# Two blocks on one core: half of x's rows and all of the context's turned by VectorE and ScalarE instead of TensorE

## The reference

```
# first block
u = rmsnorm(x);  proj = u @ w_in
y_f = fourier_mix(proj[:, :1024])            # 4 groups, DFT over positions and channels, then w_fourier
y_a = dilated_attention(q, k, v)             # 8 heads of 128
x = x + concat(y_f, y_a) @ w_out
x = x + square(relu(rmsnorm(x) @ w_up)) @ w_down;   x = rmsnorm(x)
# second block
mod = silu(c) @ w_mod + b_mod                # shift, scale and gate; one set for x, one for the context
hc = rmsnorm(ctx) * (1 + sc1c) + sh1c;  k, v, gates of the context = hc @ w_in2   -> start states
hx = rmsnorm(x) * (1 + sc1) + sh1;      q, k, v, g, low rank, cb, cc, cx = hx @ w_in2
mix = concat(gla(q, k, v, gates, states) * silu(g), cb * conv3(cc * cx)) @ w_out2
x = x + gt1 * mix;   x = x + gt2 * swiglu(modulated rmsnorm(x));   out = rmsnorm(x)
```

## Time and profile before

| what | value |
|---|---|
| median of 3 runs | 2249.17 us (2249.11 to 2249.85) |
| the profiled execution's own time | 2250.41 us |
| its span | 2248.7 us |
| granted TensorE clock | 0.998 of full |
| TensorE, VectorE, ScalarE busy | 99%, 73%, 51% of the span |
| last feed-forward chunk's steps 16 to 31, ScalarE's and VectorE's | about 926 to 1022 us |
| context's blocks k, l, v0, v1 on TensorE | 1021.9 to 1097 us |
| x's blocks on TensorE | 1097 to about 1420 us |

### The profile page before, as it was taken

One profiled execution on the slowest core, in us unless ns is written; L12 is line 12 of the kernel. 1 busy time (PEld: TensorE's weight loads), 2 busy tenths in 40 slices (PEclk: granted clock), 3 DMA queues, 4 the chain that ended last, 5 costly groups with the idle time before them and its releaser, 6 DMA issues.

```text
span 2248.7 us, 28778 instructions
## 1 busy us (share of the span) xinstructions
PE 2230.3 (99%) x10115; PEld 1841.4 (82%) x10115; DVE 1642.7 (73%) x2156; ACT 1149.5 (51%) x1500; POOL 226.6 (10%) x369
## 2 busy tenths in 40 slices
PE   9999999999999999999999999999999999999998
PEld 7888888888888888888878877878888888888886
DVE  7998789988988988998788774656555545555556
ACT  5446457446546645645565744544443344434444
POOL 0111001111111111111011000001110011100110
PEclk9999999999999999999999999999999999999999
DMA  8983678988887898887678663656665666655663
GB/s 310 325 270 123 207 249 297 326 275 296 293 303 271 277 314 279 276 275 259 219 238 256 224 198 113 226 168 203 209 198 191 220 197 203 206 189 189 207 192 124
DMA packets 250109, 527.97 MB, mean 235 GB/s; under 512 B 22258, under 2 KB 22658, under 8 KB 248704
## 3 DMA queue, kind: packets, MB, share of 16 engines
q1 hardware_dynamic: 214256, 405.32, 54.7%
q0 software_dynamic: 33776, 116.17, 15.0%
q10 hardware_dynamic: 1952, 4.85, 0.6%
HBM read 517.87 MB, written 4.21 MB: 232 GB/s over the span
## 4 chain that ended last, share of the span: by engine, by line
PE 96%; DVE 2%; ACT 1%; issue 0%; DMA 0%; ACTq 0%; DVEq 0%; POOLq 0%
PE acc L1981 30%; PE acc L1985 30%; PE acc L1990 30%; PE tp L2053 1%; DVE wlo L1176 1%; PE acc L2004 0%; PE acc L2009 0%; PE acc L2014 0%; PE tp L2367 0%; PE tp L2385 0%; PE tp L2379 0%; PE acc L2037 0%; PE acc L2036 0%; PE acc L2035 0%; PE m L2174 0%
## 5 line engine op out<-in xcount | busy, mean ns | idle before, releaser
L609 ACT ACTIVATE whi<-wring 128x1024 fp32r<-128x1024 f32 x756 | 796.4, 1060 | 930.9 <-PE acc L1990 929.7
L1176 DVE TENSOR_TENSOR wlo<-wring,whi 128x1024 fp32r<-128x1024 f32 x754 | 909.6, 1225 | 439.5 <-ACT whi L609 438.2
L1981 PE MATMUL acc<-whi,xhi 128*128 128x512 f32 x2056 | 556.1, 392 | 0.1
L1985 PE MATMUL acc<-whi,xlo 128*128 128x512 f32 x2056 | 549.8, 389 | 0.0
L1990 PE MATMUL acc<-wlo,xhi 128*128 128x512 f32 x2056 | 549.7, 389 | 0.0
L1985 PEld LDWEIGHTS acc<-whi,xlo 128*128 128x128 f32 x2056 | 386.0, 188 | 80.7
L1990 PEld LDWEIGHTS acc<-wlo,xhi 128*128 128x128 f32 x2056 | 386.0, 188 | 80.4
L1981 PEld LDWEIGHTS acc<-whi,xhi 128*128 128x128 f32 x2056 | 383.2, 188 | 82.4 <-issue 4.7
L1218 DVE SCALAR_TENSOR_TENSOR macc<-mring,csil,macc 128x512 f32<-128x512 f32 x480 | 344.3, 749 | 36.0 <-DMA mring<-w_mod 30.1
L493 POOL DMA_DIRECT2D mring<-w_mod x192 | 139.2, 725 | 1101.2 <-DVE macc L1218 1054.2
L1981 PE MATMUL acc<-whi,ahi 128*128 128x512 f32 x608 | 163.5, 391 | 0.0
(11 more groups left out here) (296 smaller groups left out, 1335.2 us busy)
## 6 DMA issues: line engine op xcount, KB each, us to landing
wring<-w_up SPq DMA_DIRECT2D x216, 512.0 KB, 5.0
wring<-w_down SPq DMA_DIRECT2D x216, 512.0 KB, 5.7
mring<-w_mod POOLq DMA_DIRECT2D x192, 512.0 KB, 5.5
wring<-w_in SPq DMA_DIRECT2D x184, 512.0 KB, 5.0
wring<-w_gate SPq DMA_DIRECT2D x88, 512.0 KB, 4.4
wring<-w_out SPq DMA_DIRECT2D x64, 512.0 KB, 5.0
tmpT<-blk POOLq DMA_DIRECT2D x128, 32.0 KB, 3.2
gbig<-ctx_in POOLq DMA_DIRECT2D x2, 1024.0 KB, 6.5
```

The source lines that it names most:

```text
L609: act.activation(whi[:, piece_slot(c, piece), 0:half], wring[:, g4, piece * half:(piece + 1) * half], ACT.Copy).then_inc(hi_done, 1)
L1176: dve.tensor_tensor(wlo[:, h4, 0:half], wring[:, g4, piece * half:(piece + 1) * half], whi[:, h4, 0:half].bitcast(F32), ALU.subtract).then ...
L1981: pe.matmul(acc[:, 2 * pair + t, :], hi[:, tile, t * P:(t + 1) * P], whi[:, h4, w], start=(tile == starts), stop=False)
L1985: pe.matmul(acc[:, 2 * pair + t, :], lo[:, tile, t * P:(t + 1) * P], whi[:, h4, w], start=False, stop=False)
```

## The change

The context's eight banks and four of x's eight are no longer turned on TensorE. Instead VectorE transposes 32x32 blocks of four tiles at a time (`turn_ctx`, `half_turn`), ScalarE moves 16 pieces of 32 partitions to their places (`move_ctx`, `half_move`), VectorE applies scale and shift in SBUF (`set_ctx`, `half_set`), ScalarE rounds the four tiles (`round_ctx`, `half_round`) and VectorE writes their remainder (`split_ctx`, `half_split`). The context's four sets start at steps 16, 20, 24 and 28, and the last one ends behind k's first two groups. x's tiles 0 to 7 are still turned on TensorE, one bank behind each group from (v0, 2) to (v1, 1); tiles 8 to 15 are turned in h's memory from (v0, 1) to (cc0, 1). TensorE waits for `ctx_lo` at k, and for `row_lo` ahead of groups 2 and 3 of cc0. The convolution's second half moves from (l, 1) and (v0, 2) to (k, 3) and (l, 0), with its strips closer together. The first head's scaling on ScalarE moves ahead of the store of the last projection block.

Of the diff, the changed lines (declarations of semaphores and of views left out):

```
...
+        ctx_pairs = tmpT[:, :, :].rearrange("p a n -> p (a n)"), ctx_placed[:, :]
+        ctx_places = [pair.rearrange("p (k t i b) -> p i k t b", k=KG, t=T, i=4) for pair in ctx_pairs]
+        ctx_tiles = [pair.rearrange("p (k s) -> p k s", k=KG) for pair in ctx_pairs]
+        ctx_strips = strips.rearrange("p j (k t b) -> p j k t b", k=KG, t=T)
...
-        CTX_TURNS = {g: b for b, g in enumerate((20, 22, 24, 25, 26, 28, 29, 30))}
-        BESIDE = ({("k", 0): (("half_norm", 0, 0, 0),), ("k", 1): (("mid_norm", 0, 0, 0),),
+        CTX_TURNED = {16: 0, 20: 1, 24: 2, 28: 3}
+        CTX_MOVES = {17: ((0, 0),), 18: ((0, 1), (0, 2)), 19: ((0, 3),), 21: ((1, 0),), 22: ((1, 1), (1, 2)), 23: ((1, 3),),
+                     25: ((2, 0),), 26: ((2, 1), (2, 2)), 27: ((2, 3),), 29: ((3, 0),), 30: ((3, 1), (3, 2)), 31: ((3, 3),)}
+        CTX_SET, CTX_ROUNDED, CTX_SPLIT = {20: 0, 25: 1, 28: 2}, {21: 0, 26: 1, 29: 2}, {22: 0, 26: 1, 30: 2}
+        BESIDE = ({("k", 0): (("ctx_set", 0, 3, 0), ("ctx_hi", 0, 3, 0), ("half_norm", 0, 0, 0)), ("k", 1): (("ctx_lo", 0, 3, 0), ("mid_norm", 0, 0, 0)),
-                   ("l", 0): (("x_squares", 0, 2, 4),), ("v0", 0): (("x_norm", 0, 0, 0), ("shift_sum", 0, 0, 0)), ("v0", 2): (("x_turn", 0, 0, 0),),
-                   ("v0", 3): (("x_turn", 0, 1, 0), ("x_turn", 0, 2, 0)), ("v1", 0): (("x_turn", 0, 3, 0),),
-                   ("v1", 1): (("x_turn", 0, 4, 0), ("x_turn", 0, 5, 0)), ("v1", 2): (("x_turn", 0, 6, 0), ("x_turn", 0, 7, 0))}, {})
+                   ("l", 0): (("x_squares", 0, 2, 4),), ("v0", 0): (("x_norm", 0, 0, 0), ("shift_sum", 0, 0, 0)), ("v0", 1): (("half_turn", 0, 0, 0), ("half_move", 0, 0, 0)),
+                   ("v0", 2): (("x_turn", 0, 0, 0), ("half_turn", 0, 1, 0), ("half_move", 0, 0, 1)),
+                   ("v0", 3): (("x_turn", 0, 1, 0), ("half_move", 0, 0, 2), ("half_move", 0, 0, 3)),
+                   ("v1", 0): (("x_turn", 0, 2, 0), ("half_set", 0, 0, 0), ("half_move", 0, 1, 0)),
+                   ("v1", 1): (("x_turn", 0, 3, 0), ("half_round", 0, 0, 0), ("half_move", 0, 1, 1)),
+                   ("v1", 2): (("half_split", 0, 0, 0), ("half_move", 0, 1, 2)), ("v1", 3): (("half_move", 0, 1, 3),)}, {})
-            ("cc0", 0): (("stack_gates", 0, 0, 0),), ("cc0", 1): (("beyond", 0, 0, 0),),
+            ("cc0", 0): (("half_set", 0, 1, 0), ("half_round", 0, 1, 0), ("stack_gates", 0, 0, 0)),
+            ("cc0", 1): (("half_split", 0, 1, 0), ("beyond", 0, 0, 0)),
...
-            ("cb1", 2): (("conv_place", 1, 2, 1),), ("cb1", 3): (("conv_place", 1, 2, 2),),
-            ("k", 0): (("conv_place", 1, 2, 3), ("conv_turn", 1, 3, 0)), ("k", 1): (("conv_place", 1, 3, 0),),
-            ("k", 2): (("conv_place", 1, 3, 1),), ("k", 3): (("conv_place", 1, 3, 2),),
-            ("l", 0): (("conv_place", 1, 3, 3),), ("l", 1): (("conv", 1, 1, 0),), ("v0", 2): (("conv", 1, 1, 1),),
+            ("cb1", 2): (("conv_place", 1, 2, 1), ("conv_place", 1, 2, 2)), ("cb1", 3): (("conv_place", 1, 2, 3),),
+            ("k", 0): (("conv_turn", 1, 3, 0),), ("k", 1): (("conv_place", 1, 3, 0), ("conv_place", 1, 3, 1)),
+            ("k", 2): (("conv_place", 1, 3, 2), ("conv_place", 1, 3, 3)), ("k", 3): (("conv", 1, 1, 0),),
+            ("l", 0): (("conv", 1, 1, 1),),
...
                         exponentials(0)
+                        scale_probs(0)
...
+            def scale_probs(hd):
+                act.wait_ge(den_inverted, hd + 1)
+                act.activation(probs[:, S:2 * S], probs[:, S:2 * S], ACT.Copy,
+                               scale=arden[:, hd, 1:2]).then_inc(probs_scaled, 1)
...
-                act.wait_ge(den_inverted, s)
-                act.activation(probs[:, S:2 * S], probs[:, S:2 * S], ACT.Copy,
-                               scale=arden[:, s - 1, 1:2]).then_inc(probs_scaled, 1)
+                else:
+                    scale_probs(s - 1)
...
+            def move_ctx(n, strip):
+                if strip == 0:
+                    act.wait_ge(ctx_turned, T * (n + 1))
+                    if n == 0:
+                        act.wait_ge(relu_lo, KG * MLP_MOVED * MLP_CHUNKS)
+                    elif n >= 2:
+                        act.wait_ge(ctx_lo, n - 1)
+                for i in range(4):
+                    placed_rows = act.activation(ctx_places[n % 2][32 * strip:32 * strip + 32, i],
+                                                 ctx_strips[32 * i:32 * i + 32, strip], ACT.Copy)
+                placed_rows.then_inc(ctx_moved, 1)
+            def round_ctx(n):
+                act.wait_ge(ctx_set, n + 1)
+                act.activation(ahi[:, 4 * n:4 * n + 4, :], ctx_tiles[n % 2], ACT.Copy).then_inc(ctx_hi, 1)
...
                     round_groups(1)
-                    if last and g in CTX_TURNS:
-                        round_modulated(ahi, CTX_TURNS[g], CTX_TURNS[g] + 1)
+                    if last and g in CTX_ROUNDED:
+                        round_ctx(CTX_ROUNDED[g])
+                    for n, strip in CTX_MOVES.get(g, ()) if last else ():
+                        move_ctx(n, strip)
...
+                elif kind == "half_move":
+                    if b == 0:
+                        act.wait_ge(row_turned, T * (a + 1))
+                    for i in range(4):
+                        placed_rows = act.activation(conv_places[a][32 * b:32 * b + 32, i],
+                                                     conv_strips[a][32 * i:32 * i + 32, b], ACT.Copy)
+                    placed_rows.then_inc(row_moved, 1)
+                elif kind == "half_round":
+                    act.wait_ge(row_set, a + 1)
+                    act.activation(xhi[:, 8 + 4 * a:12 + 4 * a, :], conv_tiles[a], ACT.Copy).then_inc(row_hi, 1)
+                        act.wait_ge(row_lo, 2)
...
+            def turn_ctx(n):
+                if n == 0:
+                    dve.wait_ge(u_done, T)
+                    dve.wait_ge(relu_moved, 4 * MLP_MOVED * MLP_CHUNKS)
+                else:
+                    dve.wait_ge(ctx_moved, 4 * n)
+                for t in range(T):
+                    rows = u_g[:, t, n * NB:(n + 1) * NB]
+                    dve.transpose(turned[:, t], rows.rearrange("p (k j b) -> p k j b", k=KG, j=4)).then_inc(ctx_turned, 1)
+            def set_ctx(n):
+                dve.wait_ge(ctx_moved, 4 * (n + 1))
+                for k in range(KG):
+                    tile = ctx_tiles[n % 2][:, k, :]
+                    set_tile = dve.tensor_scalar(tile, tile, ctx_gain(KG * n + k), ctx_shift(KG * n + k), ALU.mult, ALU.add)
+                set_tile.then_inc(ctx_set, 1)
+            def split_ctx(n):
+                dve.wait_ge(ctx_hi, n + 1)
+                dve.tensor_tensor(alo[:, KG * n:KG * (n + 1), :], ctx_tiles[n % 2],
+                                  ahi[:, KG * n:KG * (n + 1), :].bitcast(F32), ALU.subtract).then_inc(ctx_lo, 1)
...
                             set_gain1()
-                    if last and g in CTX_TURNS:
-                        modulate_bank(CTX_TURNS[g], ctx_gain, ctx_shift)
+                    if last and g in CTX_TURNED:
+                        turn_ctx(CTX_TURNED[g])
+                    if last and g in CTX_SET:
+                        set_ctx(CTX_SET[g])
                         done += n
-                    if last and g in CTX_TURNS:
-                        remainder_bank(ahi, alo, CTX_TURNS[g])
+                    if last and g in CTX_SPLIT:
+                        split_ctx(CTX_SPLIT[g])
...
+                elif kind == "half_turn":
+                    dve.wait_ge(u_done, 3 * T)
+                    dve.wait_ge(spill_s, 16)
+                    for t in range(T):
+                        rows = u_g[:, t, D // 2 + a * NB:D // 2 + (a + 1) * NB]
+                        dve.transpose(conv_turns[a][:, t], rows.rearrange("p (k j b) -> p k j b", k=KG, j=4)).then_inc(row_turned, 1)
+                elif kind == "half_set":
+                    dve.wait_ge(row_moved, 4 * (a + 1))
+                    for k in range(KG):
+                        tile = conv_tiles[a][:, k, :]
+                        kt = KT // 2 + KG * a + k
+                        set_tile = dve.tensor_scalar(tile, tile, x_gain(kt), x_shift(kt), ALU.mult, ALU.add)
+                    set_tile.then_inc(row_set, 1)
+                elif kind == "half_split":
+                    dve.wait_ge(row_hi, a + 1)
+                    tiles = slice(8 + 4 * a, 12 + 4 * a)
+                    dve.tensor_tensor(xlo[:, tiles, :], conv_tiles[a], xhi[:, tiles, :].bitcast(F32),
+                                      ALU.subtract).then_inc(row_lo, 1)
...
-            def mlp_chunk(first=False, last=False):
-                def turn_ctx(g):
-                    if last and g in CTX_TURNS:
-                        turn_rows(u_g, 1, CTX_TURNS[g])
+            def mlp_chunk(first=False):
...
                             turn_rows(blk, 2)
-                        turn_ctx(4 * j + kg)
                     multiply(hi, lo, (3,), 4, pair)
```

(33 more changed lines are left out.)

## The result

| | kernel before | changed kernel |
|---|---|---|
| median of 5 runs | 2249.85 us (2249.11 to 2251.09) | 2260.91 us (2258.81 to 2261.15) |
| ratio to before, 95% interval | | 1.0045 (1.0033 to 1.0056) |
| profiled execution and its span | 2250.41 and 2248.7 us | 2261.12 and 2259.4 us |

A forecast was written before the change was run, and what follows sets the result against it. TensorE, busy 99% of the span, was taken as the bound; -5.7 - 0.3 + 0.5 + 8.5 + 0.2 + 0 = +3.2 us gave 2252.4 us on the median. Range 2243 to 2257, likeliest case 2250 to 2255.

The forecast's parts named there:

- twelve banks and the 0.3 us stall: TensorE: eight context banks (3.9 us) and four of x (1.8 us) go, with the 0.3 us stall: -6.0.
- context late: Last chunk's steps 16 to 31, then k: late remainders at step 25 and k/3, +0.5 us, bounds 0 to +3.9.
- half of x late: v0/1 to cc0/3: hand-over chain through ScalarE and VectorE makes TensorE late by 8.5 us, bounds 0 to +9.9.
- convolution: Second half moved to k/3 and l/0: old stalls go (-2.4), low rank's split late (+2.5), sum +0.2 us.
- first head's scaling: First mixer: the 1.3 us stall moves to the Fourier product, gain 0, at best -1.3 us.
- 5.03 us, 2.3 of it waiting: Second half of x: what a step with an x bank costs ScalarE, 5.03 us, of which 2.3 is waiting.
- Rival 1: Hand-overs hidden in ScalarE's gaps, only transposes and stalls count: 2241 to 2244 us, chance 0.18.
- +2.5: Convolution: VectorE has the low rank's split at 1276.1, TensorE's gate product asks at 1273.59, so 2.5 us late.
- The granted clock is at the upper level, 2.4 GHz, over the whole span: Kernel before: claimed TensorE's clock stays at 2.4 GHz throughout the profiled span.
- Rival 2: Context half bound by VectorE, the eight banks' 3.9 us lost: 2255.8 us, chance 0.25.
- VectorE over 95% busy: Last chunk's second half: a sign expected if the forecast holds.

The follow-up runs named there:

- experiment 3: Changed kernel with x's last remainder moved to cc0/0: 2253.62 us (1.0010); then also ScalarE's strips ahead of the rounding of x's bank: 2247.68 us (0.9986).
- Experiment 2: Changed kernel with unread matmuls ahead of TensorE's two longest waits: 42 and 18 took 2262.28 us (1.0050), 22 and 10 took 2256.44 us (1.0026).
- experiment 5: Kernel before with the context's part alone, its remainders at steps 22, 26 and 30 ahead of the mod operations: 2247.53 us (0.9984).
- e7_moves_first: Changed kernel with x's last remainder at cc0/0 and ScalarE's strips of v0/2 to v1/1 ahead of the rounding of x's bank: 2247.68 us (0.9986).
- e8_conv_apart: Kernel before with the convolution's third part moved forward as in the change and its last part put at v1/1: 2248.75 us (0.9990).
- e6_split_first: Changed kernel with the remainder of x's last four tiles at cc0/0, ahead of the gate weights' stacking and four mod operations: 2253.62 us (1.0010).
- e3_order: Kernel before with only the convolution's second half and the first head's scaling moved forward, all turns as before: 2252.11 us (1.0006).
- e2_half_x: Kernel before with only the second half of x turned by VectorE and ScalarE: 2260.85 us (1.0046).

## Why the prediction was wrong

Its direction was right (no gain, a little slower) and its size was not: +3.2 forecast, 10.1 by the ratio (11.1 by the medians) measured.

| step of the sum | forecast | measured |
|---|---|---|
| twelve banks and the 0.3 us stall | -6.0 | 48 matmuls fewer, stall gone; at 0.45 for a bank, as the starts have it: -5.7 |
| context late | +0.5 | waits of 1.7 (wlo) and 0.2 (alo): +1.9 |
| half of x late | +8.5 | waits of 3.0 (whi) and 5.4 (xlo): +8.4 |
| convolution | +0.2 | -2.3, wait of 2.4: +0.1 |
| first head's scaling | 0 | 1.3 gone, 0.4 and 0.7 new: -0.2 |
| slow matmuls behind the two long waits | not in the sum | +1.8 and +1.6 |
| what a wait costs beyond its length | not in the sum | +1.4, worked out as what is left |
| outside the changed stretches | not in the sum | +0.4 in the opening, +1.0 from the last feed-forward part on |
| sum | +3.2 | +10.7 (spans) |

The starts of the same matmuls in the two traces say where it was lost. The third column is how much later, or earlier, the matmul at the end of the stretch starts than before, less the same at its beginning:

| stretch, and the starts at its end, before and after | forecast | measured |
|---|---|---|
| opening, to the first turned bank of h (7.17 and 7.54) | 0 | +0.4 |
| first mixer, to the Fourier product (195.63 and 195.93) | 0 | -0.1 |
| context, to v0/3 (1066.04 and 1065.32) | -3.9 + 0.5 | -1.0 |
| half of x, to behind the slow sets (1115.41 and 1123.61) | -1.8 - 0.3 + 8.5 | +8.9 |
| convolution, to behind the scores (1329.94 and 1339.68) | +0.2 | +1.5 |
| the rest, to the end of the span (2248.7 and 2259.4) | 0 | +1.0 |

- **Half of x.** The walk of the chain came out at 8.4 us against 8.5, with the places as foretold: 3 us in front of v1/2 to cc0/0, 5.4 in front of cc0/3. That the chain waits inside ScalarE's steps ("5.03 us, 2.3 of it waiting") was right, and experiment 3 shows that this waiting and VectorE's order were the cause: with other orders the same work fits. Rival 1 ("the strips slip into its gaps") fell for the change as it is; in the strips' other order they do.
- **The convolution.** "+2.5" was 2.4, and both old waits went. Its step was right but for the slow sets behind the wait.
- **First failed step: what a wait costs.** The sum took a wait at its length. Behind 5.4 and 2.4 us of idle time the clock stood at 1.2 GHz (0.50), and the first matmuls took 1.8 and 1.6 us longer (the two sets at 1120.03 and 1121.90 take 3.58 from start to start, the next two like them 1.84; the product and two sets at 1284.44 take 3.61 up to 1288.05, between 1291.69 and 1293.73 the same work takes 2.04). Experiment 2 shows the cause. That is 3.4 of the 7.5 us that were missing; of these, the 1.6 behind the shorter wait hang on chance, as experiment 3 shows. The prediction leaned on "The granted clock is at the upper level, 2.4 GHz, over the whole span". The table of the kernel before gives 0.998 as the mean over the span, and the sentence is false. The kernel before has slow sets of its own where the last feed-forward part starts, behind waits of 1.1, 1.5 and 1.2 us in close order (TensorE's timeline, and a stretch of the span):

```profile
1515.55 2.07 PE L2004 MATMUL acc<-whi,xhi 128*128 128x512 f32 x4 [1.20 <-ACT xhi L653]
1517.43 1.72 PE L2009 MATMUL acc<-wlo,xhi 128*128 128x512 f32 x4
1516.00:1518.00 2.00, 2.00 (x6) 1.52 (x6) 1.90 (x3) 2.00 (x3) 0.00 (x0) 0.50 0.02 4
```

So the price of a slow clock stood in the trace before the change.
- **Second failed step: "I take +0.5" for the context.** The place was right (the weights' remainder made at step 25 is the one that is late, 1.31 us at 995.15), the size was not: the walk gave VectorE's operations their lengths and its loads none. VectorE waited 4.5 us for the mod loads in place of 1.5, and experiment 5 points to this as what made it late. Rival 2 said that VectorE is bound there and all 3.9 us are lost. It isn't so: the context alone is not slower than before, and VectorE is busy for 90.3 us of 926 to 1022, as before; what grew is its waiting for mring. The sign "VectorE over 95% busy" did not come: it is 94%. That is 1.4 us by the waits, and 2.4 by the starts. Up to 0.8 us of it is chance: other executions of the same code wait 0.9 to 1.3 us for wlo in place of 1.7.
- **Scaling.** The stall moved to the Fourier product, as foretold, and in part to a score, which was not.
- **What a wait costs beyond its length.** The profile counts a wait from the end of the matmul ahead of it, 0.39 us long, but the next one would have started 0.23 us after its start; and a first set behind the shorter waits takes 1.15 to 1.21 us in place of 1.07. With 0.16 and 0.1 us for each, nine new waits and four old ones gone are 1.3 us, as an estimate, of the 1.4 that are left. The sum had no term for it.
- **Outside the changed stretches.** In the opening, eight small matmuls take 1.89 us in place of 1.44. Where the last feed-forward part starts, the stretch of 0.50 is longer in this execution: sets of 2.07, 1.91 and 1.48 us in place of 2.07, 1.72 and 1.08. That part's code is the same in all kernels, and in two of the experiments' profiles (`e7_moves_first` and `e8_conv_apart`) the clock stayed at 1.00 there. So these 1.4 us differ from one execution to the next and are no cost of the change that is shown; beside `e6_split_first`, `e7_moves_first` gains 1.8 us from there to its last matmul. Medians of several executions average over this, a single profile does not.
- **What stays open.** What decides whether a wait of 2 to 2.5 us brings the clock down was not found.
- **The range.** Its top of 2257 let the worst bounds of the named terms pass for a bound of all. It lacked a term, which no adding of bounds repairs.

## What to carry to other kernels

Where TensorE is busy for 99% of the time, moving its work to half-idle engines pays only if every hand-over between them keeps ahead of it; write down for each engine what stands in its queue in front of the late operand, and put what is ready ahead of what must wait. Price a wait of TensorE at a little more than its length, and reckon with another 1.5 to 2.7 us for one of 2 us or more: the clock may fall there, and need not. Look for stretches of a low clock in the trace before the change; a mean of 0.998 over the span hid one here. When work leaves an in-order queue, look at the loads whose latency it had covered.

## What the runs showed of the hardware

- The granted clock fell to 0.50 during waits of TensorE of 5.4 and 3.8 us, during or just behind waits of 2.4 us in three kernels (changed, `e3_order`, `e7_moves_first`) and behind one of 2.04 us (`e2_half_x`). It stayed at 1.00 for a wait of 2.41 us (`e6_split_first`) and one of 2.07 us (changed). In the kernel before it fell where waits of 1.1, 1.5 and 1.2 us stood close together. The sets of four matmuls behind took up to 2.08 us in place of 1.07, and each such fall cost 1.5 to 2.7 us beyond the wait.
- Unread matmuls of 128x128 in fp32 took 0.227 us each, two records for one, and kept the clock at 1.00; that by itself was worth 1.6 to 1.7 us in front of one wait.
- With the context's modulating and splitting no longer between its mod operations, VectorE's waits for mring between 950 and 1040 us rose from 1.3 to 1.5 us in five kernels to 3.4 to 4.5 in six, with VectorE busy for 90 of 96 us either way.
